# Four pieces of the third block's modulation formed in the second output projection, and bias rows loaded into three rotating tiles

## The reference, cut to what matters

```
shift, scale, gate = adaln(c, w_ada, b_ada)          # silu(c) @ w_ada + b_ada, 3 x 1024 columns
h = rms_norm(x, norm_g) * (1 + scale) + shift        # first block: a layer norm
u = h @ w_in
...
y = concatenate([y_a, y_b]) * silu(z)
x = x + gate * (y @ w_out)                           # first block: followed by a layer norm
```

## Time and profile before

| | us |
|---|---|
| median of 3 runs | 5650.27 (5645.52 to 5653.03) |
| the profiled execution, its own time | 5650.12 |
| its span, first to last instruction | 5648.3 |
| TensorE busy | 4959.2 (88%) |
| the first norm of "p1" | from about 37 to 217 |
| the stage "o2" | from about 4077 to 4294 |

### The profile page before, as it was taken

How to read it: one execution, slowest core, us unless ns; L and a number is a source line. 1 busy time by engine, 2 the same in 40 slices (tenths; PEclk the granted TensorE clock), 3 DMA queues, 4 the chain that set the end, 5 groups by cost and what they waited for, 6 DMA issues and landing times. The chain is left out here.

```text
span 5648.3 us, 123211 instructions
## 1 busy us (share of the span) xinstructions
PE 4959.2 (88%) x53121; PEld 3808.5 (67%) x53121; DVE 3389.7 (60%) x5239; ACT 1862.1 (33%) x3105; POOL 1317.1 (23%) x1186
## 2 busy tenths in 40 slices
PE   4799999788886885779999659999897999979989
PEld 1588888677776874667888424444486888766667
DVE  4246656344455885676992568888755000258877
ACT  2234444333334541224111324444413000126642
POOL 2201111222220000233000027677635211000012
PEclk7899999899998998889999879999998999979999
DMA  6334434221212104653231520000165211220135
GB/s 221 120 121 156 154 138 155 99 68 54 71 54 79 51 20 147 204 155 105 106 112 67 202 64 21 18 18 16 60 207 146 71 72 70 104 94 33 41 122 161
DMA packets 446664, 561.71 MB, mean 99 GB/s; under 512 B 82782, under 2 KB 337770, under 8 KB 434106
## 3 DMA queue, kind: packets, MB, share of 16 engines
q1 hardware_dynamic: 376060, 365.75, 21.0%
q10 hardware_dynamic: 54766, 130.88, 6.1%
q0 software_dynamic: 15312, 57.45, 2.6%
HBM read 350.86 MB, written 203.12 MB: 98 GB/s over the span
## 5 line engine op out<-in xcount | busy, mean ns | idle before, releaser
L164 PE MATMUL p_bank<-p_hT_high,p_w_high 128*128 128x512 f32 (+1 forms) x2744 | 1036.9, 378 | 8.1 <-PEq L37 7.7
L166 PE MATMUL p_bank<-p_hT_high,p_w_low 128*128 128x512 f32 (+1 forms) x2744 | 1029.1, 375 | 0.0
L165 PE MATMUL p_bank<-p_hT_low,p_w_high 128*128 128x512 f32 (+1 forms) x2744 | 1028.9, 375 | 0.0
L164 PEld LDWEIGHTS p_bank<-p_hT_high,p_w_high 128*128 128x128 f32 x2744 | 517.1, 188 | 109.7 <-issue 17.5
L166 PEld LDWEIGHTS p_bank<-p_hT_high,p_w_low 128*128 128x128 f32 x2744 | 516.9, 188 | 93.8
L165 PEld LDWEIGHTS p_bank<-p_hT_low,p_w_high 128*128 128x128 f32 x2744 | 517.0, 188 | 91.5
L3006 POOL TENSOR_TENSOR at_acc<-at_acc,at_p 128x512 f32<-128x512 f32 x256 | 414.6, 1620 | 124.8 <-ACT at_p L2942 102.2
L2942 ACT ACTIVATE at_p<-at_sc 128x1024 f32<-128x1024 f32 (+1 forms) x296 | 284.4, 1012 | 379.4 <-PE at_sc L2833 362.3
L3048 DVE TENSOR_REDUCE at_mx<-at_mb 128x2 f32<-128x1024 f32 (+1 forms) x280 | 342.1, 1222 | 51.4 <-PE at_mb L2844 51.2
L164 PE MATMUL o_bank<-o_w_high,o_m_high 128*128 128x512 f32 x800 | 314.4, 393 | 65.9 <-POOL o_m_low L158 65.9
L1607 PE MATMUL rsc_db<-rsc_W,rsc_TK 64*64 64x64 f32 x8640 | 298.5, 223 | 31.1 <-issue 29.7
(11 more groups left out here) (432 smaller groups left out, 10053.0 us busy)
## 6 DMA issues: line engine op xcount, KB each, us to landing
pT<-p_o ACTq DMA_DIRECT2D x128, 256.0 KB, 2.1
rwkv_chunks<-p_arr POOLq DMA_DIRECT2D x54, 512.0 KB, 5.4
o_z<-pT SPq DMA_DIRECT2D x50, 512.0 KB, 5.6
o_y<-y SPq DMA_DIRECT2D x50, 512.0 KB, 6.6
pT<-p_eo ACTq DMA_DIRECT2D x96, 256.0 KB, 2.0
rsc_X<-rwkv_chunks SPq DMA_DIRECT2D x54, 320.0 KB, 3.1
x<-o_o ACTq DMA_DIRECT2D x32, 512.0 KB, 2.8
o_x<-x SPq DMA_DIRECT2D x32, 512.0 KB, 4.6
```

The lines of the kernel that those rows point to most:

```text
L164: nc.tensor.matmul(out, lhs[0], rhs[0], start=start, stop=False)
L165: nc.tensor.matmul(out, lhs[0], rhs[1], start=False, stop=False)
L166: return nc.tensor.matmul(out, lhs[1], rhs[0], start=False, stop=stop)
```

## The change

Four pieces of the third block's modulation (columns 0 to 1535) leave the first norm and are formed in "o2". The first norm then has eleven pieces. There, the bias is loaded straight into one of three output tiles, to which VectorE adds the four groups; VectorE waits for the bias instead of for the store before, and SP waits before the bias of piece q until the store of piece q-3 has landed.

In "o2", SP issues the weights and bias of pieces 0 to 3 at the ends of its steps t = 3, 5, 13 and 15. TensorE forms pieces 0 and 1 between tiles 9 and 10, and pieces 2 and 3 between tiles 15 and 16; its loop becomes three loops. VectorE adds up pieces 0 and 1 after finishing tile 10, and 2 and 3 after tile 16. ACT issues the stores of pieces 0 and 1 at its step 11 and those of 2 and 3 after its last tile. Two tiles that were allocated without use in this kind of projection are gone.

```
@@ norm_project
-    PIECES = [(l, c * MC, MC) for l in range(2) for c in range(3 * D // MC)][:12] if later else []
-    PIECES += [(2, c, min(MC, 3 * D - c)) for c in range(2 * D, 3 * D, MC)] if later else []
+    PIECES = [(0, c * MC, MC) for c in range(3 * D // MC)] if later else []
+    PIECES += [(1, c, min(MC, 3 * D - c)) for c in range(2 * D, 3 * D, MC)] if later else []
...
-                mb = [s1.sb(f"mb{u}", [2, MC]) for u in range(2)]
-                mo = s1.sb("mo", [2, MC])
+                mo = [s1.sb(f"mo{u}", [2, MC]) for u in range(3)]
...
-                        if q >= 2:
-                            sp.wait_ge(mo_full, q - 1)
-                        sp.dma_start(mb[q % 2][:, 0:n], later[l][3][c:c + n].partition_broadcast(2)).then_inc(mw_full[q % 2], 16)
+                        if q >= 3:
+                            sp.wait_ge(mo_out[q % 3], q // 3 * 16)
+                        sp.dma_start(mo[q % 3][:, 0:n], later[l][3][c:c + n].partition_broadcast(2)).then_inc(bias_in[q % 3], 16)
...
                         dve.wait_ge(mw_free, q + 1)
-                        if q:
-                            dve.wait_ge(mo_out[(q - 1) % 2], (q + 1) // 2 * 16)
+                        dve.wait_ge(bias_in[q % 3], (q // 3 + 1) * 16)
@@ out_project, sync
+                def load_piece(q):
+                    if q >= 2:
+                        sp.wait_ge(mod_sum, q - 1)
+                        sp.wait_ge(mod_out[q % 2], q // 2 * 16)
+                    sp.dma_start(mo[q % 2][:], later[3][q * MC:(q + 1) * MC].partition_broadcast(2)).then_inc(mw_full[q % 2], 16)
+                    sp.dma_start(mw[q % 2][:], later[2].rearrange("(p k) n -> p k n", k=KT)[:, :, q * MC:(q + 1) * MC]).then_inc(mw_full[q % 2], 16)
...
                 for t in range(N):
                     if t + 3 < N:
                         load_yz(t + 3)
                     if t + 2 < N:
                         load_x(t + 2)
+                    if later and t in (3, 5, 13, 15):
+                        load_piece((3, 5, 13, 15).index(t))
@@ out_project, tensor
+                if later:
+                    rest(2, HALFWAY // 2 - 1)
+                    pieces(0)
+                    rest(HALFWAY, (N - HALFWAY) // 2 - 1)
+                    pieces(2)
+                    rest(N - 2, 1)
+                else:
+                    rest(2, N // 2 - 1)
@@ out_project, vector
                     finish(t)
+                    if later and t in (HALFWAY, N - 2):
+                        biased(0 if t == HALFWAY else 2)
+                        biased(1 if t == HALFWAY else 3)
```

More of the change, by code:

```diff
@@ L843, in _ @@
                             send(t - 2)
-                    for u in range(2 if later else 0):
-                        pool.wait_ge(mo_out[u], 16 * ((len(PIECES) - u + 1) // 2))
+                    for u in range(3 if later else 0):
+                        pool.wait_ge(mo_out[u], 16 * len(range(u, len(PIECES), 3)))
                 @block.vector
@@ L1147, in _, with out_project @@
                     act.wait_ge(e_out[u], 16 * len(range(u, 5 * M if conv else len(UNITS), NO)))
-def out_project(nc, name, yT, zT, w, parts, kind, gain, bias):
+def out_project(nc, name, yT, zT, w, parts, kind, gain, bias, later=None):
     a = ALPHA if kind == "ln" else 1.0
@@ L1172, in out_project @@
         ps = s.banks(4)
+        MC, NM, HALFWAY = 384, 4 if later else 0, 10
+        if later:
+            cond, cond_act = s.sb("cond", [P, 2, KT]), s.sb("cond_act", [P, KT, 2])
+            mw, mo = [s.sb(f"mw{u}", [P, KT, MC]) for u in range(2)], [s.sb(f"mo{u}", [2, MC]) for u in range(2)]
+            mp = [ctx.enter_context(nc.psum_tensor(f"{name}_mod{u}", [P, NT], F32)) for u in range(2)]
+            cond_in, act_ready, mw_full = s.sem("cond_in"), s.sem("act_ready"), s.sems("mw_full", 2)
+            mod_sum, mod_full, mod_out = s.sem("mod_sum"), s.sem("mod_full"), s.sems("mod_out", 2)
         w_full, w_high, w_split = s.sems("w_full", KT), s.sem("w_high"), s.sem("w_split")
@@ L1229, in _ @@
                 silu(2)
+                if later:
+                    act.wait_ge(cond_in, 32)
+                    nc.scalar.activation(cond_act[:].rearrange("p k r -> p r k"), cond[:], ACT.Silu).then_inc(act_ready, 1)
                 for t in range(N):
@@ L1232, in _ @@
                         silu(t + 3)
+                    if later and t == HALFWAY + 1:
+                        store_piece(0)
+                        store_piece(1)
                     if kind != "plain":
@@ L1237, in _ @@
                     act.dma_start(tiles[t][2][tiles[t][1] * P:(tiles[t][1] + 1) * P, :], o[t % 2][:]).then_inc(o_out[t % 2], 16)
+                for q in range(2, NM):
+                    store_piece(q)
                 for u in range(2):
                     act.wait_ge(o_out[u], 16 * len(range(u, N, 2)))
+                    if later:
+                        act.wait_ge(mod_out[u], 16 * NM // 2)
             @block.tensor
@@ L1255, in _, with pieces, rest @@
                     mm.then_inc(y_full, 1)
[L1256 to L1259, removed]
-                        for k in range(KT):
-                            mm = products(u, k)
-                        mm.then_inc(y_full, 1)
+                def pieces(q0):
+                    for q in range(q0, q0 + 2):
+                        pe.wait_ge(act_ready, 1)
+                        pe.wait_ge(mw_full[q % 2], (q // 2 + 1) * 32)
+                        if q >= 2:
+                            pe.wait_ge(mod_full, q - 1)
+                        for k in range(KT):
+                            mm = nc.tensor.matmul(mp[q % 2][QUARTERS[k % 4], 0:MC], cond_act[:, k, :], mw[q % 2][:, k, :], start=(k < 4), stop=(k >= KT - 4))
+                        mm.then_inc(mod_sum, 1)
+                def rest(first, count):
+                    with pe.Fori(0, count) as i:
+                        for u in range(2):
+                            pe.wait_ge(m_split, i * 2 + u + first + 1)
+                            pe.wait_ge(res_ready, i * 2 + u + first - 1)
+                            for k in range(KT):
+                                mm = products(u, k)
+                            mm.then_inc(y_full, 1)
+                if later:
+                    rest(2, HALFWAY // 2 - 1)
[5 more added lines that the diff above has]
+                    rest(2, N // 2 - 1)
             @block.gpsimd
@@ L1321, in finish, with biased @@
                         nc.vector.scalar_tensor_tensor(o[u][:], r[u][:], sd[u][:], gain_r[:], ALU.mult, ALU.mult).then_inc(o_full, 1)
+                def biased(q):
+                    dve.wait_ge(mod_sum, q + 1)
+                    for part in QUARTERS[0:3]:
+                        link(nc.vector.tensor_tensor(mo[q % 2][:], mp[q % 2][part, 0:MC], mo[q % 2][:], ALU.add))
+                    nc.vector.tensor_tensor(mo[q % 2][:], mp[q % 2][QUARTERS[3], 0:MC], mo[q % 2][:], ALU.add).then_inc(mod_full, 1)
                 mix(0)
```

29 lines of the change are left out of this document (17 added, 12 removed).

## The result

The changed kernel takes 5658.9 us (median of 20 runs, 5647.8 to 5672.9), the kernel before 5650.6 (20 runs, 5644.0 to 5657.1): a ratio of 1.0014, with a 95% interval of 1.0008 to 1.0020. That is 8 us longer, inside 0.2% and inside the range of the prediction's text (5631 to 5659), at its very end; but the kernel is slower beyond the interval, where 4 us less were forecast.

A forecast was written before the change was run, and what follows sets the result against it. The prediction took VectorE's waits for stores and tokens to bound the first norm, and TensorE "o2". The norm's 25 us less and "o2"'s 21 more made -4 against 5650.1: forecast 5646 us, range 5631 to 5659.

The forecast's parts named there:

- "o2", a new wait: In "o2", TensorE waits 14.5 us after tile 15 for piece 3's late-issued weights; in all 21 us more.
- the parts called hidden: In "o2", VectorE's additions, weight traffic and conditioning loads lie behind other work; the last stores cost 0 to 0.5 us.
- The first norm, the step after the change: In the first norm, the tokens' wait sets the pace once the stores' wait goes: 8.3 us a step with weights.
- L + 3.0: First norm's step: tokens' landing L, plus 1.93 us from statistics to normalisation, 0.81 for that and 0.3 for longer ones.
- lead: In the first norm, the time by which a piece's weights are issued before the tokens; 3.3 to 3.5 us forecast.
- the longest waits name no engine as releaser, so none of them bounds the step: In the first norm, VectorE's longest waits named no releasing engine, so no engine was taken to bound the step.
- L = 9.3 less 1.1 times the lead: The line for the tokens' landing under weights in the first norm, from landings of 4.9, 7.0 and 4.0 us.
- Five steps to tile 16 have none: In the first norm, the five steps after tile 11 have no weights in flight: 6.6 us each, 33.0 together.
- Small terms: In the first norm, 1 us less from fewer small loads at the start and 2 us less behind tile 16.
- The rule that was weighed: In the first norm, queues share DMA evenly: landing near 5 us, step near 8, sum about 2 us lower.
- another wait takes over: Second rival, 18 in 100: norm steps with weights stay near 9.3 us; 18 less, 21 to 24 more, 5653 to 5656.

The follow-up runs named there:

- e6: The changed kernel run again, unaltered: 1.0005 of the kernel before (0.9996 to 1.0014).
- e2: The changed kernel with pieces 2 and 3 of "o2" loaded at SP's steps 12 and 13 instead of 13 and 15: 0.9974 of the kernel before.
- e9: The changed kernel with POOL's low split of a tile in the first norm cut into four operations: 1.0000 of the kernel before.
- e10: The changed kernel with e9's split in four parts and e2's earlier loads together: 0.9972 of the kernel before.
- e14: The kernel before with POOL's low split in the norm in four parts: tile 3 to 16 took 124.5 us; no total time given.
- e11: The same kernel as e2, run again beside e10 on the same chip: 0.9983 of the kernel before.
- e5: The changed kernel with ScalarE instead of VectorE normalising each tile in the first norm: 1.0018 of the kernel before.
- e1: The changed kernel with the first norm's normalisation taking its columns in the order 0, 512, 1, 513: 1.0012 of the kernel before.

## Why the prediction was wrong, by its own steps

**"o2", a new wait: right.** Weights issued 5.5 us behind tile 15 (5.4 forecast), used 9.2 later (9.1), piece 3 at the slow clock 2.7 (2.7), then 1.4 lost over the first ten matmuls of tile 16 (their starts span 4282.99 to 4286.47, 3.48 where the full clock needs 2.07; 0.9 forecast), pieces 0 and 1 2.8 (2.9). That makes 21.6, and the stage's first wait of TensorE happened to be 1.2 shorter (18.2 against 19.4): 20.4 measured, 21 forecast. That last 1.2 is luck: in e6 it is the second wait that is as much shorter. e2 shows that the late issue made the whole pause. The sum leaves nothing over for the parts called hidden.

**"The first norm, the step after the change": this step failed.** It made the step L + 3.0, the 3.0 holding 0.81 us for the normalisation and 0.3 for the longer ones. Means over the seven steps from tile 4 to tile 11; "tokens" is from the end of a normalisation to the next statistics, "lead" as in the prediction:

| | step | normalisation | tokens | lead |
|---|---|---|---|---|
| forecast | 8.3 | 1.1 | 5.3 | 3.3 to 3.5 |
| changed | 8.8 | 2.2 | 4.7 | 4.9 |
| changed, again (e6) | 8.8 | 2.2 | 4.7 | 4.7 |
| split in parts (e9) | 8.4 | 1.1 | 5.4 | 3.0 |
| split in parts (e10) | 8.5 | 0.9 | 5.7 | 2.9 |

The fault is the 0.3. The prediction saw that some normalisations took 2.08 and priced them as an average, when the length of the longer ones depended on how the normalisation stands to POOL's split, which is just what the change moves. And "the longest waits name no engine as releaser, so none of them bounds the step" was wrong in kind: being held by POOL is no wait in the profile. e9 and e10 show it by taking the hold away: the normalisation and the step come out near the forecast. e14 shows that the same edit brings nothing in the kernel before.

The table shows one thing more. The hold adds 1.1 us to a normalisation but only 0.3 to 0.4 to a step, since a longer step gives a longer lead and so an earlier landing. The prediction's own terms say so: with L = 9.3 less 1.1 times the lead, and a lead of one step less 4.8, a step is 8.4 with a normalisation of 1.1 and 8.9 with one of 2.2 (an estimate from those two lines). Over the seven steps the miss is 3.4 us.

**"Five steps to tile 16 have none": the larger miss.** 33.0 forecast, 39.2 measured. The same loop kept its hold for three more tiles without weights; then the normalisation came early enough to be over when the split began, and the last two steps took 7.0 and 6.6. e10 has 33.8 for these five, e9 36.0. But e2 and e11, with the split undivided, have 35.1 and 36.8, so one profile tells this part of the hold's price only roughly.

**Small terms.** One us less at the start and two behind tile 16 were forecast; the start moved by +0.8 and -1.0 in the two profiles, which is nothing to be seen, and behind tile 16 it was 0.5 in the first (from its normalisation to the recurrence's first product, 849.9 before and 849.3 after).

The sum for the first profile: 25 forecast; less 6.2, 3.8 (with the step from tile 3 to 4) and 3.3 of small terms makes 11.7, and the traces show 12.0 and, for e6, 13.4 to 14.7. Against 20.4 in "o2" that is a loss of 6 to 8, as measured.

**The rule that was weighed**, the Trainium skill's round robin between the queues (DMA: Bandwidth & Descriptors, "Queues, rings and completion order"), would by the prediction's reading have had the landing near 5 whatever the lead. The means of the changed kernel, 4.7, are near that, and the prediction's line gives 4.0 for their lead. But the landing still goes with the lead: in e10 the tokens took 7.5 at a lead of 2.0 and 4.2 at one of 4.8. That speaks against the reading, and for the direction of the line, if not for its slope.

**Rivals.** The second, "another wait takes over", came nearest for the norm (18 less against 12 to 15) and gave 5653 to 5656, but by the wrong wait. The chances of a different wait that only meets at this pace weren't given their due. That the time lies inside the range of the text is luck in part: it does so only because the range reached beyond the second rival.

**The rule that would have helped** is on the Trainium skill's page SBUF — State Buffer, "Who interferes with whom": VectorE and GpSimd share one pair of SBUF ports under an exclusive lock, held for a whole instruction, and VectorE needs it in its mode with two ports or with two SBUF operands. The traces agree: an end 0.55 behind the split for 0.81 of work, whatever the length of the hold; 1.57 for a single column with two operands; ScalarE never held; statistics, which read one operand, 1.29 also beside POOL's cast (at 101.45 and 110.81 above); and a hold cut to one part by cutting the split. In which mode the normalisation ran, no trace shows. The 0.55 also means that the first 0.26 us or so of the 0.81 can pass while the split still runs (an estimate from these two numbers).

What stays open: why the four profiles with the same norm (changed, e6, e2, e11) differ by 5 us in tile 3 to 16 (108.0, 108.4, 104.0, 103.7). The two shorter ones have less held (12.8 and 9.2 against 17.5 and 18.2), so the phases seem to settle differently, but nothing was tried to force one. It also leaves the hold's price between 2 and 8 us in these thirteen steps.

## What to carry to other kernels

When one operation's duration varies threefold among like instances in a trace, look for what ends at the same distance behind it on another engine before pricing it; that wait has no semaphore and no entry among the waits. When a change takes away the wait that paces a loop, compute every loop through the same buffers, the free time of VectorE against GpSimd's long operations included, and cut the long operation if they will meet. And where a load is issued from a list that first waits for a tile's end, follow it to the engine that wants it at that same end: issuing it two tiles earlier was worth 15.7 us here, and no cost of it shows.

## What the runs showed of the hardware

A VectorE operation on a single column with two operands in SBUF (0.16 us alone) took 0.4 to 2.3 us when it met one of GpSimd's passes over a tile in SBUF, the low split with two operands or the cast with one (e5). A column order with a stride of 2 KB slowed the pass of VectorE from 0.81 to about 1.3 and left it as exposed to the hold as before (e1). A load of 1.5 MB, issued behind 0.5 MB of the same queue and beside 0.5 MB of another, was usable 9.2 us after its issue.
